# A hybrid pooling and attention layer: merge gates and branch projections with tokens on the partitions, the merged tile turned afterwards

## The reference, cut to what matters

```
xa, ga, q, k, v, gb, gm = split_columns(h @ w_in)
y_a = pool_mixer(xa, pool_w, pool_scale) * silu(ga)
y_b = attend(q, k, v) * silu(gb)            # keys within 128 tokens, and 256 context keys
g = sigmoid(gm)
merged = g[..., :D] * (y_a @ w_branch_a) + g[..., D:] * (y_b @ w_branch_b)
out = merged @ w_out
x_new = x + gate * rms_norm(out, norm_post_g)
```

## Time and profile before

| | us |
|---|---|
| median of 3 runs | 2373.91 (2373.19 to 2377.01) |
| the profiled execution | 2379.82 |
| its span on core 5, first to last instruction | 2378.3 |
| spans of the eight cores | 2362.0 to 2378.3 |
| TensorE busy | 95% of the span |
| ScalarE, GpSimd, VectorE busy | 48%, 42%, 40% |

### The profile page before, as it was taken

One profiled execution on the slowest core, in us unless ns is written; L12 is line 12 of the kernel. 1 busy time (PEld: TensorE's weight loads), 2 busy tenths in 40 slices (PEclk: granted clock), 3 DMA queues, 4 the chain that ended last, 5 costly groups with the idle time before them and its releaser, 6 DMA issues.

```text
span 2378.3 us, 69453 instructions; the slowest of 8 cores (2362.0 to 2378.3 us)
## 1 busy us (share of the span) xinstructions
PE 2261.5 (95%) x27874; PEld 1569.6 (66%) x27874; DVE 939.6 (40%) x2314; ACT 1139.1 (48%) x1563; POOL 1008.8 (42%) x985
## 2 busy tenths in 40 slices
PE   5775999999999999999998999999999999999998
PEld 2444766776676677667765667766766776677666
DVE  1321344434444444444434444344434444444442
ACT  2221554554455545545554545544555455445543
POOL 1221454445444444544443544454444445444543
PEclk8887999999999999999999999999999999999999
DMA  9935222222232222222223222222222222232211
GB/s 246 211 61 77 57 62 53 60 65 59 55 57 62 59 61 57 62 52 69 57 66 74 61 53 61 64 59 55 58 64 60 57 57 62 52 68 57 62 42 42
DMA packets 252377, 161.68 MB, mean 68 GB/s; under 512 B 223520, under 2 KB 231840, under 8 KB 249248
## 3 DMA queue, kind: packets, MB, share of 16 engines
q1 hardware_dynamic: 249616, 140.30, 24.8%
q0 software_dynamic: 2448, 16.94, 4.7%
HBM read 87.93 MB, written 33.56 MB: 51 GB/s over the span
## 4 chain that ended last, share of the span: by engine, by line
PE 88%; DMA 5%; DVE 2%; issue 1%; POOL 1%; ACT 1%; SPq 0%; POOLq 0%; DVEq 0%; ACTq 0%
PE pball L481 28%; PE pball L612 21%; PE pball L692 9%; PE pball L676 9%; PE pball L563 7%; PE pball L587 6%; PE pball L664 5%; DMA gg_scr<-s_mu 1%; DMA s_ybT<-s_yb 1%; PE pball L332 1%; DMA s_W<-w_all 1%; PE pball L640 1%; DMA s_hT<-s_xsb 1%; ACT s_xsb L429 1%; POOL s_Gbr L597 1%
## 5 line engine op out<-in xcount | busy, mean ns | idle before, releaser
L481 PE MATMUL pball<-s_W,s_hT 128*128 128x512 bf16 x3104 | 723.0, 382 | 13.5 <-DVE s_hT L471 9.4
L570 ACT ACTIVATE s_PT<-pball 128x1024 bf16<-128x1024 f32 x632 | 611.7, 1023 | 73.4 <-PE pball L563 73.4
L612 PE MATMUL pball<-s_hT,s_W 128*128 128x128 bf16 x10240 | 610.3, 220 | 28.6 <-DVE s_mu L668 20.0
L612 PEld LDWEIGHTS pball<-s_hT,s_W 128*128 128x128 bf16 x10240 | 579.5, 98 | 44.6 <-issue 44.3
L481 PEld LDWEIGHTS pball<-s_W,s_hT 128*128 128x128 bf16 x3104 | 289.6, 98 | 376.4 <-issue 74.1
L681 POOL TENSOR_TENSOR s_mgT<-s_mu,s_mv 128x512 bf16<-128x512 f32 x128 | 162.4, 1269 | 564.5 <-DVE s_mv L679 554.9
L573 POOL TENSOR_SCALAR_AFFINE_SELECT s_PT<-s_PT 128x1024 bf16<-128x1024 bf16 x248 | 270.8, 1092 | 141.2 <-ACT s_PT L570 135.4
L634 ACT ACTIVATE s_Tm<-pball 128x512 bf16<-128x512 f32 x256 | 153.1, 598 | 344.2 <-PE pball L612 289.8
L676 PE MATMUL pball<-s_ybT,s_Wb 128*128 128x128 bf16 x4096 | 252.2, 220 | 12.0 <-DMA s_Wb<-w_all 6.7
L676 PEld LDWEIGHTS pball<-s_ybT,s_Wb 128*128 128x128 bf16 x4096 | 235.4, 98 | 13.5 <-issue 13.5
L471 DVE TENSOR_SCALAR s_hT<-s_hT,s_gs,s_sh 128x128 bf16<-128x128 bf16 x536 | 126.7, 312 | 274.4 <-DMA s_hT<-s_xsb 274.3
(11 more groups left out here) (96 smaller groups left out, 2026.2 us busy)
## 6 DMA issues: line engine op xcount, KB each, us to landing
s_xt<-x SPq DMA_DIRECT2D x64, 512.0 KB, 3.7
y<-s_xt SPq DMA_DIRECT2D x64, 512.0 KB, 3.0
s_W<-w_all POOLq DMA_DIRECT2D x10, 1024.0 KB, 28.8
s_Wb<-w_mod SPq DMA_DIRECT2D x2, 2048.0 KB, 16.7
s_Wo<-w_mod SPq DMA_DIRECT2D x2, 2048.0 KB, 24.1
s_ropet<-rope SPq DMA_DIRECT2D x64, 64.0 KB, 3.4
s_W<-w_mod SPq DMA_DIRECT2D x2, 2048.0 KB, 27.7
s_Wo<-w_all POOLq DMA_DIRECT2D x3, 1024.0 KB, 29.9
```

Of the source, the lines that this page charges most:

```text
L481: E("pe", lambda e, c=c: e.matmul(out=pb, lhsT=hT[h3][:, c, :], rhs=W[:, nb, c, :], start=(c == 0), stop=(c == 7)), reads=[bf(f"hT{h3}_{c} ...
L570: E("act", lambda e, s=s, j=j: e.activation(out=view(PT[s], 0, [[1, 1024]]), in_=pbv(j, 0, [[1, 1024]]), func=AF.Exp, scale=0.125), reads= ...
L612: E("pe", lambda e, c4=c4, c=c: e.matmul(out=pb[:, c4 * 128:(c4 + 1) * 128], lhsT=W[:, blk, c, c4 * 128:(c4 + 1) * 128], rhs=hT[h3][:, c, ...
```

## The change

The merge gates are computed by `proj_tok`, A and B with the tokens held still (4 and 8 matmuls of 512 columns for each half), so `mu`, `mv` and their sum have tokens on the partitions. The sum goes to a tile `mg` (the free `yb`; `xsb` in the two early blocks) and a new step `do_mgT` turns each half into `mgT`: by DMA transpose from SyncE, by TensorE in the early blocks. The transpose of half 0 is emitted behind that of `kT`. The output projection moves behind the scores (next, self), the second queries and the attention gate half; its `fin`, with the store of `y`, moves behind the turn of `qT` and the pooling input. The pooling gate stays as it was.

```
             def do_gm(half, rd):
-                pb, pbb = feat_group(7 + half + 2 * rd)
+                pb, pbb = proj_tok(k, 7 + half + 2 * rd)
...
             def do_A(rd):
-                for c4 in range(4):
-                    cd = rd * 4 + c4
-                    for c in range(4):
-                        E("pe", lambda e, c4=c4, cd=cd, c=c: e.matmul(out=pa[:, c4 * 128:(c4 + 1) * 128], lhsT=Wa[:, c, cd * 128:(cd + 1) * 128],
-                                                                     rhs=pooled[:, c * 128:(c + 1) * 128], start=(c == 0), stop=(c == 3)),
+                for c in range(4):
+                    E("pe", lambda e, c=c: e.matmul(out=pa, lhsT=pooled[:, c * 128:(c + 1) * 128], rhs=Wa[:, c, rd * 512:(rd + 1) * 512],
+                                                    start=(c == 0), stop=(c == 3)),
...
-            def do_B(rd):
+            def do_B(rd, mg, mgn):
-                for c4 in range(4):
-                    cd = rd * 4 + c4
-                    for c in range(8):
-                        E("pe", lambda e, c4=c4, cd=cd, c=c: e.matmul(out=pbk[:, c4 * 128:(c4 + 1) * 128], lhsT=Wb[:, rd, c, c4 * 128:(c4 + 1) * 128],
-                                                                     rhs=ybT[:, c, :], start=(c == 0), stop=(c == 7)),
+                for c in range(8):
+                    E("pe", lambda e, c=c: e.matmul(out=pbk, lhsT=ybT[:, c, :], rhs=Wb[:, rd, c, :], start=(c == 0), stop=(c == 7)),
...
-                E("pool", lambda e: e.tensor_tensor(out=view(mgT, rd * 512, [[1, 512]]), in0=mu[:], in1=mv[:], op=ALU.add),
-                  reads=[bf("mu"), bf("mv")], writes=[bf(f"mgT{rd}")])
+                mh_ = mg[:, rd * 512:(rd + 1) * 512]
+                E("pool", lambda e: e.tensor_tensor(out=mh_, in0=mu[:], in1=mv[:], op=ALU.add),
+                  reads=[bf("mu"), bf("mv")], writes=[bf(n) for n in mgn[rd]])
+
+            def do_mgT(rd, mg, mgn):
+                turn(f"m{rd}", mgT[:, rd * 4:rd * 4 + 4, :], mg[:, rd * 512:(rd + 1) * 512], [bf(n) for n in mgn[rd]], [bf(f"mgT{rd}")])
...
+            mg = (xsb, [["xsb"], ["xsb"]]) if early else (yb, [["yb0"], ["yb1"]])
+
-            def AB(rd):
+            def AB(rd, now=True):
                 if prior:
                     prior[0](rd)
-                    prior[1](rd)
+                    prior[1](rd, *mg)
+                    if now:
+                        prior[3](rd, *mg)
 
             qk((0, "self"), (0, "c0"))
             if not early:
-                AB(0)
+                AB(0, False)
             if nk is not None:
                 do_kv(nk)
                 if not early:
                     do_kT(nk)
+            if prior and not early:
+                prior[3](0, *mg)
             issue_load(k + 2)
...
             if nk is None:
                 do_gb(0)
-            if prior and not early:
-                fin = prior[2]()
             qk((0, "next"), (1, "self"))
             if nk is not None:
                 do_q(nk, 1)
                 do_gb(0)
+            if prior and not early:
+                fin = prior[2]()
...
+            if nk is not None:
+                do_qT(nk, 0)
+                do_xa(nk)
             if fin is not None:
                 fin()
             if i == 0 and b > 0:
                 load_gate(b)
-            if nk is not None:
-                do_qT(nk, 0)
-                do_xa(nk)
...
-            late_out.append((do_A, do_B, do_out))
+            late_out.append((do_A, do_B, do_out, do_mgT))
```

More of the change, by code:

```diff
@@ L660, in do_A @@
                 pa, pab = next_bank()
-                for c4 in range(4):
-                    cd = rd * 4 + c4
-                    for c in range(4):
-                        E("pe", lambda e, c4=c4, cd=cd, c=c: e.matmul(out=pa[:, c4 * 128:(c4 + 1) * 128], lhsT=Wa[:, c, cd * 128:(cd + 1) * 128],
-                                                                     rhs=pooled[:, c * 128:(c + 1) * 128], start=(c == 0), stop=(c == 3)),
-                          reads=[bf("pooled"), bf("Wa")], writes=[pab], inc=(c == 3 and c4 == 3))
+                for c in range(4):
+                    E("pe", lambda e, c=c: e.matmul(out=pa, lhsT=pooled[:, c * 128:(c + 1) * 128], rhs=Wa[:, c, rd * 512:(rd + 1) * 512],
+                                                    start=(c == 0), stop=(c == 3)),
+                      reads=[bf("pooled"), bf("Wa")], writes=[pab], inc=(c == 3))
                 first = [bf(n) for n in ("cst", "ggT0", "ggT1", "mT0", "mT1")] if b == 0 and i == 0 else []
@@ L669, in do_A @@
                   reads=[bf(f"Tm{rd}"), pab], writes=[bf("mu")] + first)
-            def do_B(rd):
+            def do_B(rd, mg, mgn):
                 pbk, pbkb = next_bank()
-                for c4 in range(4):
-                    cd = rd * 4 + c4
-                    for c in range(8):
-                        E("pe", lambda e, c4=c4, cd=cd, c=c: e.matmul(out=pbk[:, c4 * 128:(c4 + 1) * 128], lhsT=Wb[:, rd, c, c4 * 128:(c4 + 1) * 128],
-                                                                     rhs=ybT[:, c, :], start=(c == 0), stop=(c == 7)),
-                          reads=[bf(f"ybT{c // 4}"), bf(f"Wb{rd}")], writes=[pbkb], inc=(c == 7 and c4 == 3))
+                for c in range(8):
+                    E("pe", lambda e, c=c: e.matmul(out=pbk, lhsT=ybT[:, c, :], rhs=Wb[:, rd, c, :], start=(c == 0), stop=(c == 7)),
+                      reads=[bf(f"ybT{c // 4}"), bf(f"Wb{rd}")], writes=[pbkb], inc=(c == 7))
                 E("dve", lambda e: e.scalar_tensor_tensor(out=mv[:], in0=Tm[:, 2 + rd, :], scalar=1.0, in1=pbk, op0=ALU.add, op1=ALU.mult),
                   reads=[bf(f"Tm{2 + rd}"), pbkb], writes=[bf("mv")])
-                E("pool", lambda e: e.tensor_tensor(out=view(mgT, rd * 512, [[1, 512]]), in0=mu[:], in1=mv[:], op=ALU.add),
-                  reads=[bf("mu"), bf("mv")], writes=[bf(f"mgT{rd}")])
+                mh_ = mg[:, rd * 512:(rd + 1) * 512]
[3 more added lines that the diff above has]
+                turn(f"m{rd}", mgT[:, rd * 4:rd * 4 + 4, :], mg[:, rd * 512:(rd + 1) * 512], [bf(n) for n in mgn[rd]], [bf(f"mgT{rd}")])
             def do_ybT(p):
```

## The result

The changed kernel took 2390.17 us (median of 5 runs, 2385.54 to 2391.97) against 2373.91: a ratio of 1.0064, 95% interval 1.0049 to 1.0079. A second measurement of the same kernel, beside experiments 5 to 7, gave 1.0055 (1.0042 to 1.0069). Forecast were 2393 us, slower. In some executions the cores of one die show a lower granted clock and a longer time (0.87 and 2616 us in one run of the first experiment); ratios and times here leave those out.

A forecast was written before the change was run, and what follows sets the result against it. TensorE, busy 95% of the span, was taken to bound the kernel. Middle 2.5, banks 1.5, block 1 10, ends 2.4 and 4.2, five other blocks -1.5: +19 us on 2373.9 gave 2393 us, range 2375 to 2412.

The forecast's parts named there:

- The saving, 0.41 a block: TensorE's gates, A and B streamed 512 wide save 0.41 us a block, 25 us over 60 blocks.
- The saving is eaten at the keys: Scores (next) wait for kT once the projection moves away: TensorE stalls 0.47 us less the block's margin.
- good block: Middle block whose kT landed 0.19 us or more before the projection (34 blocks, mean 0.24): gains 0.18 us.
- most blocks, some 25 us: Sign: TensorE waits at L563 for kT's DMA in most middle blocks, 0.2 to 0.8 us each, some 25 us.
- The late blocks stay late: Middle blocks with late kT were counted as before, each losing 0.35 us.
- The term of +2.5: Net change over 59 middle blocks, 59 x 0.06 - 59 x 0.02 us: the saving is used up.
- the 25 late blocks: Blocks whose kT margin before the projection lay below 0.19 us: mean -0.29, worst -1.45.
- all good: Rival: qT's turn leaves the crowd ahead of ybT, late blocks vanish; -10.6 for 2.5, 2380 us, chance 0.15.
- The merged transposes cost nothing in middle blocks: Two more transposes per block on SyncE's queue, landing before the moved projection needs them: cost nothing.
- Block 1: First entry: TensorE stops at half 0's turn until the merge add is done: +10 us, between 5 and 15.
- The ends: Last projections wait for the merged transpose: +2.4 us at the very end, 3 x 1.4 = +4.2 around entry ends.
- Banks: Every second block, scores (context 0) may wait for VectorE's scaling to free a bank: +1.5 us, bounds nothing and 4.

The follow-up runs named there:

- experiment 5: Changed kernel with merge gates, A and B streamed 128 columns wide again, order and turns kept: ratio 1.0218 to the kernel before.
- experiment 6: Changed kernel with second queries ahead of the scores, block 1's early turns later and the load of x later: 2350.8 us, ratio 0.9903 to the kernel before.
- experiment 7: Kernel of experiment 6 with the last block's merged tile turned by TensorE instead of DMA: ratio 0.9912 to the kernel before.
- the first experiment: Also experiment 1: changed kernel with the second queries moved ahead of the scores (next, self): ratio 0.9961 to the kernel before.
- experiment 8: Kernel of experiment 6 with gates, A and B streamed 128 columns wide: 2390.67 us, ratio 1.0070 to the kernel before.
- experiment 3: Changed kernel with only the turn of qT put back behind the store of y: ratio 1.0047 to the kernel before.
- Experiment 4: Changed kernel with the load of x issued later, behind the second half's B projection: ratio 1.0008 to the kernel before.

## Why the prediction was right, and where it was not

**The saving, 0.41 a block: right.** Experiments 1, 6 and 8 show it three times, as 0.42. The Trainium skill's figures for the issue gap ("TensorE: Matmul & The Clock Gate", section Back-to-back issue gap) would have made it some 10 us a block; the groups of 5.36 and 5.18 us bear out, not those figures.

**The saving is eaten at the keys: right.** A typical block gained 0.12, against 0.18 forecast for a good block, so the stall was 0.30 and not 0.23. Fewer waits have a name than I expected (19 a core, 5.5 us, for "most blocks, some 25 us"), but nearly every block does stall, 58 of 61 on core 6. The rest of the 0.30 stands in stalls too short for the list and in the slower matmuls behind them (0.62 for 0.54 and 3.56 for 3.45 in the block above), which the profile books as busy time.

**The late blocks stay late: wrong, the step that failed.** The term of +2.5, from a mean margin of 0.02 over 59 blocks, took the 25 late blocks along unchanged. Counted from the end of `pv(1)`, the keys of typical blocks land as before (15.1 us later), but 9 to 13 of 59 land 0.2 or more later than that in the changed kernel, on the eight cores, where 21 to 25 did before, and the mean fell from 15.52 to 15.31 (medians over the cores). That is 0.21 us a block, some 12 us; the middle came out at -8.0 in place of +4.0. TensorE's listed waits in middle blocks for late `ybT` and `hT` themselves fell from 6.6 us a core to 1.2. Experiment 5 shows which part of the change it needs: with the order kept and the streaming narrow again, the late blocks are back. I had read the matmul count only as time on TensorE. That the lateness comes by way of the instruction packets, which fell with the matmuls, is supported by the split by packets in each kernel, but not shown. The rival "all good" forecast such a middle, but by way of the turn of `qT`, which experiment 3 excludes.

**The merged transposes cost nothing in middle blocks: wrong by 3 to 5 us.** Half 1 lands late behind the load of `x`, which I had called harmless since nobody waits for the load. Experiment 4 shows who waits: the transpose behind it (3.0 us of waits; the middle got 5 us shorter without them). The same explains most of the entry change, +5.4 for 2.8: experiment 4 takes 4.3 of it back.

**Block 1: right** in place and cause, and 1.8 short in size (+11.8 for +10, inside its bounds of 5 and 15). The later restart is there as 2.0 and the second stand as 2.47 for 2.3; A and B of half 1, put at 0.87 + 1.73, took 4.9 at the lower clock, which the sum had named but not priced. **The ends:** +3.0 for +3.8, with waits of 2.19 and 0.94 at the last projection. **Banks:** the +1.5 did not come. No scores in a middle block of any core have a listed wait for VectorE's scaling, and on core 6 the idle time before all scores in middle blocks is 10.3 us, of which the keys account for 10.2.

So the errors, 12.0 too much for the middle, 2.6 too little at the change of entry and 1.8 too little in block 1, partly cancelled: by core medians +12.5 for +19. That the run medians differ by 16.3 brings the forecast of 2393 closer to 2390.17 than its parts deserve, and is luck.

## What to carry to other kernels

An independent group that stands between a transfer's issue and its first reader is cover: before moving one away, subtract its length from that transfer's margin, and put another independent group there (experiment 1: 0.30 us off a typical block for the exchange of two lines). A transpose that is needed soon goes ahead of a bulk load in a queue, not behind it (experiment 4). Count what a change does to the number of instructions as well as to their time.

## What the runs showed of the hardware

Small DMA transposes land late more often where a packet of the instruction queue moves at the same time: 51 of 65 over 3.0 us against 2 of 59 in the kernel before, 33 of 53 against 5 of 71 in the narrow one, 8 of 23 against 7 of 101 in the changed one; and late `ybT` went 12, 25, 39 as the packets went 145, 181, 229. Not shown is the mechanism, nor that it is the packet alone: no run changed the packets and left TensorE's stream as it was. A transpose of 128x512 queued behind a 512 KB load landed after 4.05 us in the median, with the load later after 2.30. The four score matmuls that waited for a key transpose started 0.14 us after its landing. The Trainium skill's rule to issue a DMA early and wait for it late ("DMA: Bandwidth & Descriptors", section Rules for kernel authors) agrees with experiment 1, where the wait was put later and the issue left in place.
